# Stick-breaking attention: the left-over keys of all query blocks of a head in one block

## The reference

```
def one_block(args):                       # 128 queries q_blk of every head
    visible = key_pos[None, :] < q_pos[:, None]
    z = einsum('bhqd,bhkd->bhqk', q_blk, k) * 64 ** -0.5
    log_beta = log_sigmoid(z)
    log_keep = where(visible, log_beta - z, 0.0)
    log_w = log_beta + cumsum(log_keep, axis=3, reverse=True) - log_keep
    w = where(visible, exp(log_w), 0.0)
    return einsum('bhqk,bhkd->bhqd', w, v)
```

## Time and profile before

| | us |
|---|---|
| median of three runs | 2785.77 (2778.38 to 2788.07) |
| profiled execution | 2784.55 |
| its span in the profile | 2782.6 |
| attention, from the first turn to the output projection | 1767.1 to 2032.1 of the span |
| busy over the span: PE, DVE, ACT, POOL | 2725.0, 1983.5, 1071.7, 1211.2 |

### The profile page before, as it was taken

How to read it: one execution, slowest core, us unless ns; L and a number is a source line. 1 busy time by engine, 2 the same in 40 slices (tenths; PEclk the granted TensorE clock), 3 DMA queues, 4 the chain that set the end, 5 groups by cost and what they waited for, 6 DMA issues and landing times. The chain is left out here.

```text
span 2782.6 us, 48746 instructions
## 1 busy us (share of the span) xinstructions
PE 2725.0 (98%) x19450; PEld 2494.4 (90%) x19450; DVE 1983.5 (71%) x2504; ACT 1071.7 (39%) x1994; POOL 1211.2 (44%) x1054
## 2 busy tenths in 40 slices
PE   8999999999999999999999999999999999999998
PEld 7999998888999999999999998888887888888786
DVE  5767536887468777777878444577747988888777
ACT  5222224544443332333434101477734333334433
POOL 3000015556146555656663000232233666665775
PEclk9999999999999999999999999999999999999999
DMA  4333332231302322234432425554320232335432
GB/s 127 90 92 84 95 126 96 94 112 64 95 10 100 104 100 104 88 128 163 153 127 69 143 102 167 153 122 110 85 61 31 99 114 96 102 102 189 167 132 91
DMA packets 215995, 298.40 MB, mean 107 GB/s; under 512 B 9915, under 2 KB 151372, under 8 KB 215772
## 3 DMA queue, kind: packets, MB, share of 16 engines
q1 hardware_dynamic: 205194, 257.01, 29.4%
q0 software_dynamic: 10368, 38.21, 4.0%
q10 hardware_dynamic: 210, 0.07, 0.0%
HBM read 212.08 MB, written 83.19 MB: 106 GB/s over the span
## 5 line engine op out<-in xcount | busy, mean ns | idle before, releaser
L2137 DVE TENSOR_TENSOR RL<-RAW,RH 128x512 fp32r<-128x512 f32 (+1 forms) x408 | 407.6, 1001 | 198.2 <-ACT RH L1516 197.3
L1516 ACT ACTIVATE RH<-RAW 128x512 fp32r<-128x512 f32 (+1 forms) x408 | 248.4, 618 | 679.8 <-POOL RAW L1146 283.0
L2849 PE MATMUL PS<-QP,RH 128*128 128x512 f32 x1584 | 487.9, 389 | 0.0
L2852 PE MATMUL PS<-QP,RH 128*128 128x260 f32 x1584 | 413.4, 282 | 0.0
L2851 PE MATMUL PS<-QP,RH 128*128 128x260 f32 x1584 | 413.2, 282 | 0.0
L2849 PEld LDWEIGHTS PS<-QP,RH 128*128 128x128 f32 x1584 | 297.3, 188 | 62.1 <-issue 0.2
L2849 PE MATMUL PS<-QP,RL 128*128 128x512 f32 x792 | 309.2, 390 | 2.7 <-DVE QP L2154 1.6
L2851 PEld LDWEIGHTS PS<-QP,RH 128*128 128x128 f32 x1584 | 298.8, 189 | 0.0
L2852 PEld LDWEIGHTS PS<-QP,RH 128*128 128x128 f32 x1584 | 298.3, 188 | 0.0
L1146 POOL TENSOR_TENSOR RAW<-RAW 128x512 f32<-128x512 f32 (+1 forms) x136 | 213.5, 1570 | 139.2 <-DVE RL L2137 133.9
L2414 PE MATMUL PS<-YH,WL 128*128 128x348 f32 (+1 forms) x744 | 241.6, 325 | 1.8 <-DVE WL L1769 1.8
(11 more groups left out here) (376 smaller groups left out, 6951.3 us busy)
## 6 DMA issues: line engine op xcount, KB each, us to landing
RAW<-in_ffn_w_gate_up SPq DMA_DIRECT2D x44, 1024.0 KB, 5.3
s_in<-obuf POOLq DMA_DIRECT2D x32, 520.0 KB, 4.4
raw<-in_gdn_w_in SPq DMA_DIRECT2D x32, 512.0 KB, 4.1
RAW<-in_ffn_w_down SPq DMA_DIRECT2D x16, 1024.0 KB, 5.2
QF<-s_a SPq DMA_DIRECT2D x12, 1040.0 KB, 7.9
QF<-s_a SPq DMA_DIRECT2D x12, 1024.0 KB, 7.2
s_a<-ua SPq DMA_DIRECT2D x22, 520.0 KB, 2.8
s_a<-ua SPq DMA_DIRECT2D x22, 512.0 KB, 3.3
```

Source lines behind the costliest of these rows:

```text
L1516: act.activation(m.RH[n % m.ring][:, 0:kn, :], m.weight_block(p, i), ACT.Copy).then_inc(m.f_hi[0], 1)
L2137: dve.tensor_tensor(m.RL[n % m.ring][:, 0:kn, :], m.weight_block(p, i), m.RH[n % m.ring][:, 0:kn, :].bitcast(F32), ALU.subtract).then_inc( ...
L2849: done = pe.matmul(acc, w, x, start=first, stop=last)
L2852: done = pe.matmul(acc[:, 1, :], w, x[:, 1, :], start=first, stop=last)
```

## The change

The 16 left-over keys leave the units. For each head, the last 16 queries of each of its 8 blocks (only they see left-over keys) make one tile `endQ` of 128, and one 128 x 128 score block S against the left-over keys of all blocks stands for both heads in one turn bank (`end_scores`). It is made into sigmoids (`take_ends`), masked (`end_unseen`), scanned (`end_scans`), and cut down to its own 16 x 16 blocks (`end_own`, two masks). The turn T (`turn_ends`) transposes it to `PTe` for the weighted sums and, by a product with the picking matrix `pickE`, makes `after`: a column for each block and head with the left-over keys' whole product, which the units' scans take as initial value in place of 1.0. The values of the left-over keys are packed by GpSimd (`end_values`) and turned as the last value turn. Units now have 128 (i+1) columns: big ones' scores lie in banks 0 and 1, small ones' in bank 2, and turns go round in three banks, 3 to 5, so that a turn waits for the copy of the third turn before it. Block 3 has one turn in place of two, block 7 two in place of three. S of the next pair is formed in slot 6, T in slot 9, the value turns move to slots 10, 11 and 12 (`EXTRA`). GpSimd's steps stand behind units 7, 9, 10 and 11 of the order, VectorE's end scans behind unit 9's. For pair 0 all of it stands in the query projection. Zeroing of tile tails on GpSimd is gone.

The diff, cut (tiles in SBUF, helpers of two lines and the building of `pickE` left out):

```
-TURNS = [[(0, 1)], [(0, 2)], [(0, 3)], [(0, 3), (3, 1)], [(0, 4), (4, 1)], [(0, 4), (4, 2)], [(0, 4), (4, 3)],
- [(0, 3), (3, 3), (6, 2)]]
+TURNS = [[(0, min(i + 1, 4))] + ([(4, i - 3)] if i > 3 else []) for i in range(8)]
-V_SLOT = {9: 0, 10: 1, 11: 2}
+EXTRA = {6: ("S",), 9: ("T",), 10: ("V", 0), 11: ("V", 1), 12: ("V", 2)}
...
+def turn_bank(n):
+    return 3 + n % 3
...
-    u = U % NU
-    n = META + 128 * (UNITS[u][1] + 1)
-    return {7: 232, 4: 184, 3: 1272}.get(UNITS[u][1], 0 if u % 2 == 0 else 1536), n
+    i = UNITS[U % NU][1]
+    n = 128 * (i + 1)
+    return 512 - n // 2 if i > 3 else 1024, n
...
-        last = P_of(unit)[:, n - 128:n]
+        last = P_of(unit)[:, n - 112:n]
         pool.wait_ge(t_kp, unit + 1)
         pool.affine_select(out=last, in_=last, compare_op=ALU.is_ge, fill=1.0, base=-1,
-                           pattern=[[-1, 128]], channel_multiplier=1).then_inc(t_km, 1)
+                           pattern=[[-1, 112]], channel_multiplier=1).then_inc(t_km, 1)
+    def pick_ends():
+        pool.memset(pickE[:, :], 0.0).then_inc(t_end, 1)
...
+    def end_queries(j):
+        QS = keys_of(j)[2]
+        if j:
+            pool.wait_ge(t_tr, TURN_NO["T", j - 1] + 1)
+        for h in range(2):
+            pool.wait_ge(t_load[h], 96 * (j + 1))
+            pool.tensor_copy(endQ[:, h, :].rearrange("p (i q) -> p i q", q=16), end_cols(QS[h][:, :].bitcast(F32))).then_inc(t_end, 1)
+    def end_unseen(j):
+        blocks = ends[:, :, :].rearrange("p h (i r) -> p h i r", r=16)
+        pool.wait_ge(t_ca, TURN_NO["S", j] + 1)
+        pool.affine_select(out=blocks, in_=blocks, compare_op=ALU.is_ge, fill=1.0, base=-1,
+                           pattern=[[0, 2], [-16, 8], [-1, 16]], channel_multiplier=1).then_inc(t_end, 1)
+    def end_own(j):
+        blocks = ends[:, :, :].rearrange("p h (i r) -> p h i r", r=16)
+        pool.wait_ge(t_es, 2 * j + 2)
+        pool.affine_select(out=blocks, in_=blocks, compare_op=ALU.is_ge, fill=0.0, base=0,
+                           pattern=[[0, 2], [-16, 8], [0, 16]], channel_multiplier=1).then_inc(t_end, 1)
+        pool.wait_ge(t_end, end_step(j, "own"))
+        pool.affine_select(out=blocks, in_=blocks, compare_op=ALU.is_ge, fill=0.0, base=15,
+                           pattern=[[0, 2], [16, 8], [0, 16]], channel_multiplier=-1).then_inc(t_end, 1)
+    def end_values(j):
+        pool.wait_ge(t_vload, 16 * (j + 1))
+        if j:
+            pool.wait_ge(t_tr, TURN_NO["V", j - 1, 2] + 1)
+        pool.tensor_copy(endV[:, :].rearrange("p (i q) -> p i q", q=16), end_cols(dvT_of(j)[:, META:L])).then_inc(t_end, 1)
     for l in range(23):
+        if l == 21:
+            end_queries(0)
+            pool.wait_ge(mm_chunk, P_Q.mm0 + 2 * (P_Q.jobs - 2))
+            pick_ends()
+            end_unseen(0)
+            end_own(0)
+            end_values(0)
         if l == 22:
             unseen(0)
             unseen(1)
             pool.wait_ge(mm_chunk, P_O.mm0)
-            for h in range(2):
-                pool.memset(PTb[h][:, 1024:1056], 0.0).then_inc(t_zero, 1)
-                pool.memset(PTs[h][:, 512:544], 0.0).then_inc(t_zero, 1)
             unseen(2)
         store(l)
...
-    for unit, d in zip((3, 4), dV12):
-        unseen(unit)
-        pool.memset(d[:, 0:8, 64:192], 0.0).then_inc(t_zero, 1)
-        pool.memset(d[:, 8, :], 0.0).then_inc(t_zero, 1)
+    unseen(3)
+    unseen(4)
     store(23)
     for unit in range(5, PAIRS * NU):
+        j, u = divmod(unit, NU)
         unseen(unit)
+        if j < PAIRS - 1:
+            if u == 7:
+                end_queries(j + 1)
+            if u == 9:
+                end_unseen(j + 1)
+            if u == 10:
+                end_own(j + 1)
+            if u == 11:
+                end_values(j + 1)
...
+    def take_ends(j):
+        n = TURN_NO["S", j]
+        act.wait_ge(t_tr, n + 1)
+        act.activation(ends[:, :, :], PS[:, turn_bank(n), 0:256].rearrange("p (h c) -> p h c", h=2),
+                       ACT.Sigmoid, scale=-0.125).then_inc(t_ca, 1)
+    def take_turned_ends(j):
+        n = TURN_NO["T", j]
+        act.wait_ge(t_tr, n + 1)
+        if j > 1:
+            act.wait_ge(t_pv, NU // 2 * (j - 1))
+            act.wait_ge(t_p, NU * (j - 1))
+        act.activation(after[j % 2][:, :, :], PS[:, turn_bank(n), 256:272].rearrange("p (h i) -> p h i", h=2), ACT.Copy)
+        act.activation(PTe[j % 2][:, :, :], PS[:, turn_bank(n), 0:256].rearrange("p (h c) -> p h c", h=2),
+                       ACT.Copy).then_inc(t_ca, 1)
...
+        dve.wait_ge(t_ca, TURN_NO["T", j] + 1)
         dve.wait_ge(t_km, U + 1)
         P = P_of(U)[:, 0:n][:, ::-1]
-        dve.tensor_tensor_scan(P, P, P, 1.0, ALU.mult, ALU.bypass).then_inc(t_p, 1)
+        dve.tensor_tensor_scan(P, P, P, after[j % 2][:, h, i:i + 1], ALU.mult, ALU.bypass).then_inc(t_p, 1)
+    def end_scans(j):
+        dve.wait_ge(t_end, end_step(j, "unseen"))
+        for h in range(2):
+            P = ends[:, h, :][:, ::-1]
+            dve.tensor_tensor_scan(P, P, P, 1.0, ALU.mult, ALU.bypass).then_inc(t_es, 1)
...
+                if l == P_KV.jobs + P_Q.jobs - 2 and ch:
+                    end_scans(0)
...
+        if u == 9 and j < PAIRS - 1:
+            end_scans(j + 1)
...
-        pe.wait_ge(t_vload, 16 * (j + 1))
-        if n > 1:
-            pe.wait_ge(t_ca, n - 1)
+        if n > 2:
+            pe.wait_ge(t_ca, n - 2)
         else:
             pe.wait_ge(taken, TAKEN0[P_Q] + 2 * (P_Q.jobs - 2))
-        for k in range(nb):
-            rn = META if g == 2 else 128
-            m = pe.transpose(PS[0:rn, 4 + n % 2, 128 * k:128 * k + 128],
-                             dvT_of(j)[:, 128 * (k0 + k):128 * (k0 + k) + rn], ident[:, :])
+        if g < 2:
+            pe.wait_ge(t_vload, 16 * (j + 1))
+            for k in range(nb):
+                m = pe.transpose(PS[:, turn_bank(n), 128 * k:128 * k + 128],
+                                 dvT_of(j)[:, 128 * (k0 + k):128 * (k0 + k) + 128], ident[:, :])
+        else:
+            pe.wait_ge(t_end, end_step(j, "values"))
+            m = pe.transpose(PS[:, turn_bank(n), 0:128], endV[:, :], ident[:, :])
         m.then_inc(t_tr, 1)
+    def end_scores(j):
+        KL, KH, _ = keys_of(j)
+        n = TURN_NO["S", j]
+        if j:
+            pe.wait_ge(t_ca, n - 2)
+        for h in range(2):
+            pe.wait_ge(t_end, end_step(j, "queries") + h)
+            z, q = PS[:, turn_bank(n), 128 * h:128 * h + 128], endQ[:, h, :]
+            z = z.rearrange("p (i r) -> p i r", r=16)
+            pe.matmul(z, q, end_cols(KL[h][:, META:L]), start=True, stop=False)
+            m = pe.matmul(z, q, end_cols(KH[h][:, META:L]), start=False, stop=True)
+        m.then_inc(t_tr, 1)
+    def turn_ends(j):
+        n = TURN_NO["T", j]
+        pe.wait_ge(t_ca, n - 2)
+        pe.wait_ge(t_end, end_step(j, "own") + 1)
+        for h in range(2):
+            pe.matmul(PS[:, turn_bank(n), 256 + 8 * h:264 + 8 * h], pickE[:, :], ends[:, h, 0:128:16], start=True, stop=True)
+        for h in range(2):
+            m = pe.transpose(PS[:, turn_bank(n), 128 * h:128 * h + 128], ends[:, h, :], ident[:, :])
+        m.then_inc(t_tr, 1)
...
-        if n < 5:
-            pe.wait_ge(taken, TAKEN0[P_Q] + 2 * P_Q.jobs - 4 + n)
-        pe.wait_ge(t_ca, n - 1)
+        if turn_bank(n) > 3 and n < 8:
+            pe.wait_ge(taken, TAKEN0[P_Q] + 2 * P_Q.jobs - (turn_bank(n) == 5))
+        pe.wait_ge(t_ca, n - 2)
         pe.wait_ge(t_p, U + 1)
         P = P_of(U)
         for k in range(nb):
-            m = pe.transpose(PS[:, 4 + n % 2, 128 * k:128 * k + 128], P[:, 128 * (k0 + k):128 * (k0 + k) + 128], ident[:, :])
-        if n == last_turn(U):
-            m = pe.transpose(PS[:, 4 + n % 2, 128 * nb:128 * nb + 128], P[:, 128 * (i + 1):128 * (i + 2)], ident[:, :])
+            m = pe.transpose(PS[:, turn_bank(n), 128 * k:128 * k + 128], P[:, 128 * (k0 + k):128 * (k0 + k) + 128], ident[:, :])
         m.then_inc(t_tr, 1)
...
-            m = pe.matmul(PS[64 * h:64 * h + 64, bank, c0 + 96:c0 + 128], V[:, i + 1, 192 * h:192 * h + 64],
-                          P[h][:, r0:r0 + 32], start=False, stop=True, tile_position=(0, 64 * h))
+            m = pe.matmul(PS[64 * h:64 * h + 64, bank, c0 + 112:c0 + 128], V[:, 8, 192 * h:192 * h + 64],
+                          E[:, h, 16 * i:16 * i + 16], start=False, stop=True, tile_position=(0, 64 * h))
...
-        if parts > 2:
-            turn(U, 2)
-        if u in V_SLOT and j < PAIRS - 1:
-            turn_values(j + 1, V_SLOT[u])
+        if u in EXTRA and j < PAIRS - 1:
+            extra(j + 1, *EXTRA[u])
...
                 scores(0)
                 scores(1)
+                turn_ends(0)
                 turn_values(0, 2)
-                pe.wait_ge(t_ca, 2)
+                pe.wait_ge(t_ca, 3)
...
                 if ph is P_Q and m == P_Q.jobs - 2 and ch:
+                    end_scores(0)
                     turn_values(0, 0)
```

(63 more changed lines are left out.)

37 lines of the change are left out of this document (15 added, 22 removed).

## The result

The changed kernel takes 2798.38 us (median of four runs, 2797.03 to 2801.11) against 2783.14 (four runs) before on the same chip: ratio 1.0052, 95% interval 1.004 to 1.0064. It is slower by half a per cent, where 2789.5 was forecast. The profiled execution has 2798.45 us, its span 2796.7: 14.1 us more than the span of before.

The account below looks back on a forecast made before the run. TensorE bounds the kernel before; the keys' ring paces pairs after. From 2784.55 us: +1.3 projection, +4.5 pair 0, +1.5 clock, +2.4 ring, -4.7 last pair give 2789.5; own range 2783 to 2797, over all 2773 to 2803.

Parts of the forecast that it names:

- a ring through the keys' landing: Pairs 1 to 6: value load, keys landed, S, T, next value load take 33.05 us against 32.64, +2.4 in all.
- wait at S: TensorE in each pair waits about 2.3 us for S, ended by GpSimd's copies, which wait for a key DMA.
- one at T: TensorE's wait before T: T starts at 25.35 us after the value load, 0.85 us after TensorE could take it.
- (c): Rival: the wait for S recurs and lowers the clock in each pair, 2795 or 2805 us; chance 0.28, between 2793 and 2806.
- keys landed: Step from value load to a pair's keys being loaded: 17.7 us, from 18.1 in the earlier trace less 0.4.
- Removed and added instructions: TensorE's work in a pair: 1.76 us of transposes and 0.3 of shorter units removed, 1.35 added.
- Bank waits: Waits for ScalarE's copies out of turn banks: up to 2.0 us a pair removed by the third bank.
- 29.9 us a pair: A pair's length on TensorE by work and bank waits alone, from 32.64 us before.
- Last pair: No S, T or value turns there: 19 transposes and bank waits go from 38.15 us, -4.7 us.
- Pair 0: First pair: S waits for its loads, slot 12 ends 4.5 us later, plus 1.5 us for a lowered clock.
- Masks held: GpSimd's masks for T meet VectorE's scan 10 and end only with it: first at 24.8 us, second at 25.3.
- (b): Rival: keys are there when S comes, the ring does not close, a pair takes 31.2 us, 2771 in all; chance 0.15.

Follow-up runs that it names:

- ScalarE's order as before: Changed kernel, but ScalarE takes unit 14's first turn behind its sigmoid for unit 16, as before the change: 2798.04 us, ratio 1.0046 to the kernel before.
- the kernel without them: Changed kernel with S, T and value turns in later slots, key loads before value load, ScalarE copying no turn ahead of a sigmoid: 2773.07 us, ratio 0.9958.
- three small edits: Each alone on the changed kernel: key loads before value load (1.0036), VectorE waiting for T's masks before scan 10 (1.0041), ScalarE's old order for unit 14 (1.0046).
- keys first: Changed kernel with a pair's key and query loads ahead of its value load in SP's queue: 2795.86 us, ratio 1.0036 to the kernel before.
- the first run: Changed kernel, but a turn waits for the copy of the turn before the last, as with two banks: 2799.26 us, ratio 1.0055 to the kernel before.

## Why the prediction was too low

Its mechanism held: a ring through the keys' landing paces pairs 1 to 6, with a wait at S ended by GpSimd's copies and one at T ended by a mask held by scan 10. The loads sent 2.0 us later, which made a pair 2.0 us longer, and S and T moved alone, which took both waits and 2.85 us a pair, show it. The size did not hold: 2798.38 lies in the range over all but above the forecast's own (2783 to 2797), and the wait at S, which was to be 2 us or more in each pair, was that in one of six. The sum was 7 us short in its own terms, and the untouched stages added 2.3; the range over all held it because it was drawn wide for (c), whose mechanism did not come, and so far that is luck.

- **Ring, +2.4 forecast, +5.8 measured.** The step "keys landed" was mis-sized: 17.7 us after the value load was taken from the DMA share of the earlier trace rows, and GpSimd's last copy was to be done at 18.15; it starts at 18.6, S's second head at 18.96 for 18.25. The DMA share was read a microsecond early. SyncE's last key load of that pair in the kernel before (first row below) took 11.3 us from issue to landing (second row): it landed at 1880.5, 19.0 us after the value load and not 18.1, and less the 0.4 that is the 18.6 measured. The rest was near: S to T 6.82 for 7.1, T to the next value load 7.67 for 7.7. That makes 33.45 for 33.05; a pair whose S waited 2.06 us brings the mean to 33.60. TensorE comes to S at 17.6, not 15.9: 1.3 us are waits that I did not have, for score banks and for a scan. They cost little there (0.5 us of them was worth 0.25 in the run with ScalarE's order as before) and mostly made the wait at S look smaller (1.0, not 2.3). The other 0.4 us is not broken down.

```profile
1869.23 0.60 SPq L905 DMA_DIRECT2D KHe<-s_kh  x1
```

```profile
KHe<-s_kh SPq DMA_DIRECT2D x1, 260.0 KB, 11.3
```

- **Work, two errors that nearly cancel.** Removed and added instructions were to give 0.7 us a pair; TensorE's busy time fell by 1.3. Bank waits were to give 2.0; they gave at most 0.9, because that is all the idle time that TensorE had in a pair. The 1.8 and 0.2 us of the earlier trace rows are waits of weight loads, which run beside matmuls still in flight; TensorE's own wait in that pair is 0.8. So 29.9 us a pair was forecast without waits and 30.36 measured in the kernel without them.
- **Last pair, -4.7 forecast, -1.7 measured.** Here TensorE itself waited 2.7 us for copies before and still waits 1.1, so that term gave 1.6 of its 2.0; what the sum lacked is 2.7 us of new waits for score banks (1.3) and scans (1.4), with no ring to hide them.
- **Pair 0, +6.0 forecast, +7.0 measured.** Loads landed later than forecast: the second copy starts 21.5 us after the value load, where they were to land at 20, and S's second head comes 1.2 us late. The clock was at 0.50, its lower level of 1.2 GHz, for 13.5 us (the stretch above) in which TensorE was busy 8.65. S to T took 8.59 us (1792.53 to 1801.12) where 7.1 and 1.5 for the clock were forecast, and 6.82 in the pair at full clock. So the clock's price was as forecast, but not its cause: the clock fell before the wait at S, which starts at 1788.04, in a stretch in which TensorE waited 1.28 and 0.86 us for scans (second row below; the column is the third from the end). In the kernel before the clock falls in pair 0 too (first row), which the prediction overlooked. What a pair 0 at full clock would take in either kernel stays open.

```profile
1776.20:1779.60 3.40, 3.40 (x30) 2.94 (x31) 1.67 (x3) 1.07 (x2) 1.63 (x4) 0.50 1.08 352
```

```profile
1783.00:1786.40 3.40, 2.16 (x11) 1.90 (x12) 2.85 (x3) 0.84 (x2) 1.90 (x2) 0.77 1.03 220
```

- **Masks held.** The first of T's masks took 1.95 us beside a scan of 1.79 and 0.51 free. The Trainium skill's rule (SBUF — State Buffer, Who interferes with whom), that a VectorE instruction with two SBUF inputs contends with a GpSimd instruction that reads SBUF, agrees on that side: with VectorE held back the mask took 0.51 us and T's wait went. It gave 0.1 to 0.25 us a pair, since the ring's next wait took the rest.
- **Rivals.** The time lies in (c)'s range, not by its mechanism: after pair 0 the clock stays at 1.00 in the changed kernel's profiled execution. But its price is real: with 3.0 us or more of wait at S it fell in five of six pairs. (b)'s 31.2 us a pair is what the kernels with S and T later come near or beat (31.35, 30.75, 30.36), by another place of S, not by faster keys.

## What to carry to other kernels

When a new step consumes a transfer earlier than before, draw the ring (issue, landing, use, release, issue) and compare its length with the pair's work before counting any saving; if the ring is longer, much of what is saved elsewhere comes back as a longer wait. First move the consumer, then shave: three small edits inside the closed ring gave 0.06 to 0.16% of the time, within or near the width of the intervals, S two and T four slots later 0.86%. And what a bank wait costs is the idle time of the matmuls, not the waits of the weight loads.

## What the runs showed of the hardware

- The clock does not follow from one wait's length alone. With 3.0 to 3.5 us of idle at S it fell in five of six pairs and not in one (3.17 us); in the run with ScalarE's order as before it fell to a mean of 0.75 over 6.8 us at waits of 2.80, 1.96 and 1.66 us, and not at 1.64, 1.54 or 1.46; with the keys first it fell in one pair behind a wait of 1.41 us at T, and not in three others behind 1.40, 1.41 and 1.55; in the changed kernel a wait of 2.06 us left it at 1.00.
- A plain copy on GpSimd of 128 x 128, 0.29 us when free, is held like a masking: 1.28 us beside VectorE's subtraction of 1.20 (keys first), and 1.59 beside a scan of 2.06 in pair 0 of the changed kernel (rows below).
- A third PSUM bank for turns was worth 0.2 to 0.3 us a pair among pairs at full clock (0.4 by the mean of the first run), where the weight loads' waits had suggested 2.0.

```profile
1783.70 1.59 POOL L1246 CAST endQ<-QSo 128x128 fp32r<-128x128 f32 x1 [0.40 <-DMA KHo<-s_kh]
```

```profile
1783.15 2.06 DVE L2401 TENSOR_TENSOR_SCAN PB<-PB,after 128x896 f32<-128x896 f32 x1
```
